# A two-block transformer kernel on one core: half-array products alternate, the convolution and silu move in the instruction order

## What is computed

```
def first_block(x, ...):
    h = rms_norm(x, norm_g)
    dq, dk, dv, dg, mq, mk, mv, mg, gates = split_in_proj(h @ w_in)
    # rope on dq, dk, mq, mk
    o_a = diff_attention(dq, dk, dv, ...) * silu(dg)        # 4 heads, two maps each
    o_b = moba_attention(mq, mk, mv) * silu(mg)             # 8 heads
    merged = sigmoid(g_a) * (o_a @ w_branch_diff) + sigmoid(g_b) * (o_b @ w_branch_moba)
    x = x + merged @ w_out
    x = x + sigmoid(x @ w_ple_gate) * (p @ w_ple)
    return rms_norm(x, final_g)

def second_block(x, ...):
    h = rmsnorm(x, ln_mix_g) * (1 + sc1) + sh1
    q, kc, vc, ksl, vsl, kw, vw, gts, cb, cc, ch = split(h @ w_in)
    # 15 compressed blocks of keys and values: gelu(window @ w1) @ w2
    o_attn = gates * (compressed, selected and window attention of q)   # 8 heads
    o_conv = cb * causal_conv3(cc * ch)
    x = x + gt1 * (concat(rmsnorm(o_attn), rmsnorm(o_conv)) @ w_out)
    h2 = rmsnorm(x, ln_ffn_g) * (1 + sc2) + sh2
    x = x + gt2 * peer_ffn(h2, ...)     # product keys, top 16 of 16384 experts per head
    return rmsnorm(x, ln_final_g)
```

## Time and profile before

| | |
|---|---|
| median of 3 runs | 1253.82 us (1251.61 to 1255.06) |
| profiled execution | 1253.62 us |
| its span in the trace | 1251.7 us, 27468 instructions |
| PE busy | 1206.2 us, 96% |
| DVE, ACT, POOL busy | 895.9, 769.7 and 568.4 us |
| chain that ended last, by engine | PE 83%, DVE 7%, ACT 4%, issue 3%, DMA 2% |

### The profile page before, as it was taken

How to read it: one execution, slowest core, us unless ns; L and a number is a source line. 1 busy time by engine, 2 the same in 40 slices (tenths; PEclk the granted TensorE clock), 3 DMA queues, 4 the chain that set the end, 5 groups by cost and what they waited for, 6 DMA issues and landing times.

```text
span 1251.7 us, 27468 instructions
## 1 busy us (share of the span) xinstructions
PE 1206.2 (96%) x8800; PEld 1110.5 (89%) x8800; DVE 895.9 (72%) x1761; ACT 769.7 (61%) x1728; POOL 568.4 (45%) x505
## 2 busy tenths in 40 slices
PE   8999999989998999999999999999999999999997
PEld 8898889988887899999999999999888888888885
DVE  5768678888666739993578888870476867676866
ACT  5445776455655555556778777875555555555555
POOL 3665444545455338988877777778300000000000
PEclk9999999999999999999999999999999999999999
DMA  6668556538643435665666776668666676767663
GB/s 238 220 219 295 194 188 216 169 119 288 228 139 105 145 119 169 185 184 169 202 203 203 216 209 195 209 204 273 193 230 231 185 254 189 263 189 260 190 195 106
DMA packets 85827, 249.84 MB, mean 200 GB/s; under 512 B 8020, under 2 KB 29693, under 8 KB 84989
## 3 DMA queue, kind: packets, MB, share of 16 engines
q1 hardware_dynamic: 77356, 209.62, 53.5%
q0 software_dynamic: 8400, 39.34, 8.5%
...
## 4 chain that ended last, share of the span: by engine, by line
PE 83%; DVE 7%; ACT 4%; issue 3%; DMA 2%; POOL 1%; DVEq 0%; ACTq 0%; SPq 0%; POOLq 0%
PE psum L675 83%; DMA ring<-v_rows 2%; ACT w_hi L1156 1%; DVE w_lo L1724 1%; DVE arena L1777 1%; DVE s_sb L1738 1%; PE psum L871 1%; DVE rstd L1718 0%; ACT arena L1139 0%; DVE h_lo L1768 0%; DVE nmax L1900 0%; ACT h_hi L1187 0%; DVE xres L1858 0%; ACT arena L1310 0%; POOL arena L1637 0%
## 5 line engine op out<-in xcount | busy, mean ns | idle before, releaser
L1554 POOL TENSOR_TENSOR w_lo<-ring,w_hi 128x512 fp32r<-128x512 f32 x368 | 496.1, 1360 | 283.6 <-ACT w_hi L1156 273.3
L1156 ACT ACTIVATE w_hi<-ring 128x512 fp32r<-128x512 f32 x734 | 445.5, 627 | 276.2 <-PE psum L675 266.7
L675 PE MATMUL psum<-h_hi,w_hi 128*128 128x256 f32 x1832 | 533.9, 291 | 26.6 <-DVE w_lo L1724 6.5
L675 PE MATMUL psum<-h_lo,w_hi 128*128 128x256 f32 x1832 | 520.1, 284 | 0.0
L675 PE MATMUL psum<-h_hi,w_lo 128*128 128x256 f32 x1832 | 520.0, 284 | 0.0
L675 PEld LDWEIGHTS psum<-h_hi,w_hi 128*128 128x128 f32 x1832 | 352.6, 192 | 40.7 <-issue 20.9
L675 PEld LDWEIGHTS psum<-h_lo,w_hi 128*128 128x128 f32 x1832 | 353.1, 193 | 0.3
L675 PEld LDWEIGHTS psum<-h_hi,w_lo 128*128 128x128 f32 x1832 | 352.9, 193 | 0.0
L1724 DVE TENSOR_TENSOR w_lo<-ring,w_hi 128x512 fp32r<-128x512 f32 x238 | 186.3, 783 | 120.3 <-ACT w_hi L1156 119.7
L675 PE MATMUL psum<-w_hi,h_hi 128*128 128x512 f32 (+1 forms) x592 | 223.1, 377 | 4.4 <-DVE arena L1746 2.1
L675 PE MATMUL psum<-w_lo,h_hi 128*128 128x512 f32 (+1 forms) x592 | 221.9, 375 | 0.0
...
## 6 DMA issues: line engine op xcount, KB each, us to landing
ring<-u_t SPq DMA_DIRECT2D x128, 512.0 KB, 3.6
ring<-v_rows SPq DMA_DIRECT2D x128, 512.0 KB, 3.9
...
```

Source lines behind the costliest of these rows:

```text
L675: return nc.tensor.matmul(out, lhs, rhs, start=start, stop=stop, **kw)
L1156: nc.scalar.activation(w_hi[:, half, :], src, ACT.Copy).then_inc(hi_done, 1)
L1554: nc.gpsimd.tensor_tensor(w_lo[:, half, :], src, w_hi[:, half, :].bitcast(F32), ALU.subtract)\
```

## The change

1. Products of the two array halves alternate. In `pv` 4 to 7 and in odd `pv` from 9 on, the inner loop runs over m. `cmpk` and `cmpv` become one PE step whose 32 products alternate, and the hidden features of the values move to the upper 64 columns and partitions. The scores of compressed keys alternate the two groups, and the route keys the two key sets.
2. The convolution is split into the steps `z` (POOL, cc times ch), `conv` (DVE) and `cgate` (POOL, times cb, then ACT's square). The fill projections come in another order, with the first one before the compression and `turn 15` and the last fills before `pv 15`. `mix 1` alternates low parts with the multiplications of the norm.
3. Silu leaves turn 3 and becomes four ACT instructions of 512 columns behind the exponents of soft 7, where the sigmoid table was loaded before; that load now comes with the first sigmoid. DVE's multiplications by silu come later (`pv` 6 does those of 4 to 6, and `subh` those of the head before).
4. `ahead` makes the parts of the next projection's weights already at a `scores` step, ahead of the mask on DVE.
5. A value projection takes each buffer when it needs it, and issues the last rotation behind the products of its first two jobs.

```diff
-FILL2 = [f"{n}{b}" for b in range(4) for n in ("cc", "ch", "cb")]
+FILL2 = ["cc0", "ch0", "cc1", "ch1", "cb0", "cc2", "ch2", "cb1", "cc3", "ch3", "cb2", "cb3"]
...
     fill = [("proj", n) for n in FILL2]
-    steps += [("scores", 8), ("gates",), ("scores", 9), ("soft", 8), ("soft", 9), ("cmpk",), ("cmpv",), fill.pop(0),
-              ("turn", 8), ("scores", 10), ("cmpk1",), ("cmpv1",), ("soft", 10), fill.pop(0), ("cmps",), fill.pop(0)]
-    for p in range(9, 15):
+    steps += [("scores", 8), ("gates",), ("scores", 9), ("soft", 8), fill.pop(0), ("soft", 9), ("cmpk",), ("cmpv",),
+              ("turn", 8), ("scores", 10), fill.pop(0), ("cmpk1",), ("cmpv1",), ("soft", 10), fill.pop(0), ("cmps",)]
+    for p in range(9, 16):
+        steps += {10: [("z", 0), ("z", 1)], 12: [("z", 2)], 14: [("z", 3)]}.get(p, [])
         steps.append(("turn", p))
...
             steps.append(("scores", p + 2))
-        steps.append(("mod", mod.pop(0)))
+        if p < 15:
+            steps.append(("mod", mod.pop(0)))
         if p + 2 < 16:
             steps.append(("soft", p + 2))
+        steps += {10: [("conv", 0)], 11: [("cgate", 0), ("conv", 1)], 13: [("conv", 2), ("cgate", 1)], 14: [("conv", 3)]}.get(p, [])
         steps.append(fill.pop(0))
...
             steps.append(("cmpt",))
-        if p % 2 == 1:
-            steps.append(("conv", (p - 9) // 2))
-        if p in (9, 12, 14):
+        if p in (9, 12):
             steps.append(fill.pop(0))
-        if p % 2 == 1:
+        if p in (9, 11, 13):
             steps.append(("pv", p))
-    steps += [("conv", 3), ("turn", 15), ("mix", 0), ("pv", 15)]
+    steps += [("cgate", 2), ("cgate", 3), ("pv", 15), ("mix", 0)]
     assert not fill
...
-            if s == ("scores", 9):
+            if s in (("scores", 8), ("scores", 9)):
...
+            if s[0] == "scores":
+                return ahead(next(x for x in STEPS[STEPS.index(s):] if x[0] == "proj"))
...
-                    while pending:
-                        rope_turn(pending.pop(0))
...
-                    out = [take(at[s + (j,)]) for j in range(jobs)]
+                    out = [None] * jobs
...
+                            if x == 0 and j == 2:
+                                while pending:
+                                    rope_turn(pending.pop(0))
+                            if x == 0:
+                                out[j] = take(at[s + (j,)])
...
-                        for m in range(2):
-                            o, at = out[DH * m:DH * m + DH, :], P * (p - 4) + DH * m
-                            mm(o, v[:, 0, at:at + DH], pt[:, m, 0:T], True, False)
-                            last = mm(o[:, P:T], v[:, 1, at:at + DH], pt[:, m, T:TRI], False, True)
+                        for i in range(TT):
+                            for m in range(2):
+                                o, at = out[DH * m:DH * m + DH, P * i:T], P * (p - 4) + DH * m
+                                last = mm(o, v[:, i, at:at + DH], pt[:, m, T * i:T + P * i], i == 0, i == 1)
...
-                            o = out[DH * m:DH * m + DH, :]
-                            mm(o, bd[:, m, (p - 8) // 2, :], cpt[:, m, :], True, False)
-                            for w, pp in ((0, pt_of(p - 1)), (1, pt)):
-                                at = P * w + DH * m
-                                mm(o, v[:, 0, at:at + DH], pp[:, m, 0:T], False, False)
-                                last = mm(o[:, P:T], v[:, 1, at:at + DH], pp[:, m, T:TRI], False, w == 1)
+                            mm(out[DH * m:DH * m + DH, :], bd[:, m, (p - 8) // 2, :], cpt[:, m, :], True, False)
+                        for w, pp in ((0, pt_of(p - 1)), (1, pt)):
+                            for i in range(TT):
+                                for m in range(2):
+                                    o, at = out[DH * m:DH * m + DH, P * i:T], P * w + DH * m
+                                    last = mm(o, v[:, i, at:at + DH], pp[:, m, T * i:T + P * i], False, w == 1 and i == 1)
...
-                elif kind in ("cmpk", "cmpv"):
-                    which = 0 if kind == "cmpk" else 1
-                    w1 = slot_ready(SLOT_AT[s])
-                    pe_.wait_ge(a_read, filled("proj", ("kc", "vc")[which]))
+                elif kind == "cmpk":
+
+                    pe_.wait_ge(a_read, filled("proj", "vc"))
...
-                    win = win_of(which)
-                    out = take_a(AT[s + (0,)])
+                    w1s = [slot_ready(SLOT_AT[(n,)]) for n in ("cmpk", "cmpv")]
+                    outs = [take_a(AT[n, 0]) for n in ("cmpk", "cmpv")]
...
-                        last = mm(out[0:DH, 0:3 * CMP_N], w1[:, l2 * DH:l2 * DH + DH],
-                                  win[:, :, 2 * l2:2 * l2 + 16 * (CMP_N - 1) + 1:16], l2 == 0, l2 == 15)
-                    last.then_inc(a_done, 1)
+                        for which in range(2):
+                            last = mm(outs[which][DH * which:DH * which + DH, 0:3 * CMP_N],
+                                      w1s[which][:, l2 * DH:l2 * DH + DH],
+                                      win_of(which)[:, :, 2 * l2:2 * l2 + 16 * (CMP_N - 1) + 1:16], l2 == 0, l2 == 15)
+                            if l2 == 15:
+                                last.then_inc(a_done, 1)
...
-                    for g in range(2):
-                        for i in range(TT):
-                            for r in range(4):
+                    for i in range(TT):
+                        for r in range(4):
+                            for g in range(2):
...
-                        for m in range(2):
-                            for j in range(4):
+                        for j in range(4):
+                            for m in range(2):
...
-                    if p in (7, 15):
-                        nc.scalar.activation(small[:, 58:60], eps_c[:, 0:2], ACT.Sigmoid if p == 7 else ACT.Sqrt)
+                    if p == 7:
+                        for b in range(0, 8, 2):
+                            pair = blk(SIL + b, 2)
+                            nc.scalar.activation(pair, pair, ACT.Silu).then_inc(gates_ready, 1)
+                    if p == 15:
+                        nc.scalar.activation(small[:, 58:60], eps_c[:, 0:2], ACT.Sqrt)
...
-                    if p == 3:
-                        nc.scalar.activation(blk(SIL, 8), blk(SIL, 8), ACT.Silu).then_inc(gates_ready, 1)
-                        nc.scalar.activation(small[:, 56:58], eps_c[:, 0:2], ACT.Exp)
...
-                elif kind == "conv" and s[1]:
-                    b = s[1] - 1
+                elif kind == "cgate":
+                    b = s[1]
+                    act.wait_ge(a_done, filled("gates"))
                     act.wait_ge(conv_done, b + 1)
                     square(blk(OT + b), blk(SQ + b), osq_done)
...
                     act.wait_ge(rstd_ready, 2 + s[1])
...
-                elif kind == "conv":
-                    for b in s[1:]:
-                        pool.wait_ge(a_read, filled("proj", f"ch{b}"))
-                        nc.gpsimd.tensor_tensor(blk(CONV + 4 + b), blk(CONV + 4 + b), blk(CONV + 8 + b), ALU.mult)\
-                            .then_inc(z_done, 1)
-                    for b in s[1:]:
-                        pool.wait_ge(conv_step, 3 * b + 3)
-                        pool.wait_ge(a_read, filled("proj", f"cb{b}"))
-                        pool.wait_ge(mod_done, MODS_B)
-                        nc.gpsimd.tensor_tensor(blk(OT + b), blk(PROD + b), blk(CONV + b), ALU.mult)\
-                            .then_inc(conv_done, 1)
+                elif kind == "z":
+                    b = s[1]
+                    pool.wait_ge(a_read, filled("proj", f"ch{b}"))
+                    nc.gpsimd.tensor_tensor(blk(CONV + 4 + b), blk(CONV + 4 + b), blk(CONV + 8 + b), ALU.mult)\
+                        .then_inc(z_done, 1)
+                elif kind == "cgate":
+                    b = s[1]
+                    pool.wait_ge(conv_step, 3 * b + 3)
+                    pool.wait_ge(a_read, filled("proj", f"cb{b}"))
+                    pool.wait_ge(mod_done, MODS_B)
+                    nc.gpsimd.tensor_tensor(blk(OT + b), blk(PROD + b), blk(CONV + b), ALU.mult).then_inc(conv_done, 1)
...
-                    p = s[1]
-                    dve.wait_ge(a_read, filled(*s))
-                    dve.wait_ge(gates_ready, 1)
-                    v.tensor_tensor(blk(OT + p), blk(OT + p), blk(SIL + p), ALU.mult).then_inc(o_ready, 1)
+                    for p in {6: (4, 5, 6), 7: (7,)}.get(s[1], ()):
+                        dve.wait_ge(a_read, filled("pv", p))
+                        dve.wait_ge(gates_ready, 4)
+                        v.tensor_tensor(blk(OT + p), blk(OT + p), blk(SIL + p), ALU.mult).then_inc(o_ready, 1)
...
-                    dve.wait_ge(sub_done, 3 * hd + 2)
-                    v.tensor_tensor(blk(OT + hd), blk(OT + hd), blk(SIL + hd), ALU.mult).then_inc(sub_done, 1)
+                    for g in ((), (0, 1), (2,), (3,))[hd]:
```

(3 more changed lines are left out.)

61 lines of the change are left out of this document (32 added, 29 removed).

## The result

The changed kernel takes 1257.23 us (1256.78 to 1258.83, nine runs), the kernel before 1253.46 (1251.11 to 1255.06, nine runs): ratio 1.0034, 95% interval 1.0023 to 1.0045. It is slower by about 4 us, and the forecast was 1247.0. The two profiled executions differ by 3.4 us of span (1251.7 and 1255.1), so the traces show where the time went.

A forecast was written before the change was run, and what follows sets the result against it. PE, busy 96% of the span, was taken as the bound, with under 50 us of gaps. Terms -1.9 - 2.2 - 1.0 - 5.1 + 1.3 - 0.6 + 2.9 gave -6.6 against 1253.6: 1247.0 us, range 1241 to 1252.

The forecast's parts named there:

- the pairs: Alternating halves overlap on PE: compression 5.26 to 2.6 us, its scores 3.34 to 1.9, pv 11 3.0 to 1.9.
- Silu's -4.3: Moving silu from turn 3 removes 2.88 us of PE waiting and a slow stretch there, -4.3 us.
- the two long waits: Ahead of cb1 and cb2, PE waits near 3.6 us each for an eviction queued behind ACT's wait for cgate.
- the slow clock after them: Behind the two waits of 3.6 us the clock falls to 0.50, together +2.9 us.
- The part up to turn 10: Second fill until turn 10: 10.4 us saved in work, waits and slow stretches, 5.3 of new waits, net -5.1.
- Rotation and low parts: Rotation inside both value projections, -1.9 us; low parts ahead of masks at the first fills, -2.2 us.
- silu: Silu's whole move: -4.3 at turn 3, +2.0 behind soft 7, +1.3 in ple, sum -1.0 us.
- six matmuls go between them: At value projections, 0.72 us of matmuls between rotations: DVE reads the second 0.47 us later, PE gains 0.95 us each.
- What is late instead is the exponents, with two fill projections to hide it: At the first fills, soft 0's exponents come one low part (0.68 us) later, hidden by fills; without cover it costs 0.7.
- The bound that I gave, 0: Least gain of the rotation in the value projections: the wait just moves, 0 us; the other bound was -2.1.
- Rival (b): Paired records overlap no more than now; compression, its scores and pv 9 give 5.1 us back: 1252.1, chance 0.14.
- (c): ACT's wait for cgate grows; 0.3% slower needs 8.8 us in each of the two waits instead of 3.6; chance 0.08.

The follow-up runs named there:

- x2: The changed kernel with the low parts behind the masks again, all else as changed: 1254.94 us, ratio 1.0017 to the kernel before.
- x13: The kernel before with the last rotation inside the value projection as the only change: 1254.59 us, ratio 1.0026 to the kernel before.
- x14: The kernel before with the low parts ahead of the masks as the only change: 1253.93 us, ratio 1.0021 to the kernel before.
- x1: The changed kernel with steps cgate 0 and 1 behind the fill and pv of p = 11 and 13: 1252.80 us, ratio 1.0006 to the kernel before.
- x3: The changed kernel with the last rotation ahead of the value projection again: 1256.37 us, ratio 1.0038 to the kernel before.
- x5: The kernel before with the alternating products alone, order of steps as before: 1256.66 us, ratio 1.0028 to the kernel before.

## Why the prediction was wrong

**Right.** What the pairs do to PE's rows (2.84, 1.97 and 1.9 for 2.6, 1.9 and 1.9). Silu's -4.3. The wait of 1.8 at turn 9 that L2011 ends (2.0 forecast) and the 1.2 ahead of cmp (1.5). The place and the chain of the two long waits: square behind POOL's product behind probabilities, and the slow clock after them. The part up to turn 10 is near, -4.1 for -5.1; its sum had both slow stretches gone (2.9), and the one from 348.0 to 351.5 stayed, which is about 1.4.

**Where the 10.0 us between forecast and trace are.** Rotation and low parts 4.8, turn 10 to the routing 3.0, silu 1.6, up to turn 10 1.0, the start, where nothing was changed, 0.7; from the routing on it is 1.1 the other way.

**Wrong, the two long waits.** 3.6 each forecast, 4.4 and 4.5 measured. The chain from the last exponent to PE was right (373.46 to 377.48: 4.0). The term that failed is the one in front, from the end of the scores to the last exponent: 6.0 forecast, and 7.1 measured (366.4 to 373.46). I had also read it off the wrong turn: the rows at 374.55 and 375.36 are turn 12 and scores 14, whose mask stood behind the convolution; for scores 13 it was 4.1 before. So what the new order puts ahead of the mask was not worth 0.5 but 3.0 us there, 1.9 for the low part and 1.1 for the taps of the convolution, and x2 shows 1.2 to 1.6 of the low part in each wait. The clock behind them cost 4.5 and not 2.9: each time it stayed at 0.50 for 6.8 us, and PE worked for 4.7 and 5.3 of them, where the stretches before were 3.4.

**Wrong, rotation and low parts (-4.1 forecast, +0.7 measured up to turn 3, apart from the 0.7 of the start).** The steps "six matmuls go between them" and "the waits go" took PE's wait away and didn't follow DVE behind it. Measured from the first projection, DVE reads the last rotation's product 0.3 us later at the first value projection and 0.1 at the second (0.47 forecast). At the first one its next low part is late (0.72); at the second the value copies stand behind modulation steps that now take 2.3 us. "What is late instead is the exponents, with two fill projections to hide it" was the wrong cover: DVE has no slack in this stretch. The traces also say which of the two did what from the first projection to turn 0: 92.1 us before, 92.4 with the rotation inside (x13), 90.9 with the low parts ahead (x14), 91.1 with both where the clock didn't fall behind the wait of 2.15 (x1), and 92.7 where it did (the changed kernel). So the low parts do bring 1.2 of the 2.2 us in their place, and lose them later; the rotation brings nothing, and costs 0.3, or 1.8 with a slow stretch. The bound that I gave, 0, excluded a loss without a reason, and x13 and x14 show losses of 0.26% and 0.21%, 3.3 and 2.6 us.

**Wrong, silu (-1.0 forecast, +0.6 measured).** Its sum took the best case of the clock: I priced the wait at soft 7 at 2.6 and left the slow stretch out. With the exponents later it was 3.35, and slow. ple took 2.0 for 1.3.

**Not seen at all.** Rival (b) had the pairs give nothing because they would not overlap. They overlap, and still cost 0.28% in the old order. No case of mine had PE getting faster and the kernel slower. Of my rivals (c), the longer waits for `cgate`, comes nearest, but needed 8.8 us each; what made up the rest were the three small parts, each a loss, which I had all booked as gains.

**Left open.** The stretch from the routing to the end differs by up to 3 us between executions whose code is the same there: 815.3 before and 813.4 in x14, 813.0 in x3 and 816.0 in x2. So the 1.7 us that it is shorter in the changed kernel, and any single difference of a few microseconds between two traces, may be no more than this. x3 and x13 differ in what the rotation costs (nothing to tell, and 0.26%); the traces show 1.8 and 0.3 us up to turn 0, the other way round, and I don't know why. No run varied the clock by itself, so how much of the 3.5 us in x5 it makes is an estimate from one trace.
